# Row order in DRAM of the staged weight halves, and a three-dimensional source for their loads

## The reference

```python
for l in range(DEPTH):                       # DEPTH = 2
    mix = mixer_sublayer(h, ..., w_in[l], ..., w_out[l])
    h = layer_norm(DEEPNORM_ALPHA * h + mix, ln1_g[l], ln1_b[l])
    ffn = grouped_moe(h, router_w, router_bias, exp_w_gate[l], exp_w_up[l], exp_w_down[l])
    h = layer_norm(DEEPNORM_ALPHA * h + ffn, ln2_g[l], ln2_b[l])
...
for e in range(N_EXPERTS):                   # grouped_moe, 16 experts
    a = jax.nn.silu(h @ w_gate[e]) * (h @ w_up[e])
    y = y + dense_gates[:, e:e + 1] * (a @ w_down[e])
...
def swiglu(h, wi, wo):                       # four times in the second stack, D_FF = 2816
    gate, up = jnp.split(h @ wi, 2, axis=-1)
    return (jax.nn.silu(gate) * up) @ wo
```

## Time and profile before

| | |
|---|---|
| median of three runs | 2252.26 us |
| profiled execution, first to last instruction (span) | 2251.1 us |
| TensorE busy | 2131.1 us (95%) |
| VectorE busy | 1547.9 us (69%) |
| ScalarE busy | 1237.7 us (55%) |
| DMA traffic | 446.81 MB, 198 GB/s on average |
| the two expert stages, roughly | 225 to 496 us and 742 to 990 us of the span |

### The profile page before, as it was taken

One profiled execution on the slowest core, in us unless ns is written; L12 is line 12 of the kernel. 1 busy time (PEld: TensorE's weight loads), 2 busy tenths in 40 slices (PEclk: granted clock), 3 DMA queues, 4 the chain that ended last, 5 costly groups with the idle time before them and its releaser, 6 DMA issues.

```text
span 2251.1 us, 32506 instructions
## 1 busy us (share of the span) xinstructions
PE 2131.1 (95%) x12234; PEld 1855.9 (82%) x12234; DVE 1547.9 (69%) x2172; ACT 1237.7 (55%) x1985; POOL 50.0 (2%) x64
## 2 busy tenths in 40 slices
PE   7988999998988999989999998999999999889999
PEld 5777888876777788868999887789999997779998
DVE  7457999996557999985654757456666666655665
ACT  4454777764544777764444565544445444554443
POOL 0000000000000000010000000000000001000000
PEclk9999999998998999999999999999999999999999
DMA  6122999992224999975555452445565555133553
GB/s 240 64 76 96 354 360 361 364 355 98 86 78 143 366 360 358 361 292 169 168 187 188 157 182 95 149 131 176 184 194 177 180 187 197 66 121 131 187 186 114
DMA packets 124215, 446.81 MB, mean 198 GB/s; under 512 B 14320, under 2 KB 15472, under 8 KB 123120
## 3 DMA queue, kind: packets, MB, share of 16 engines
q1 hardware_dynamic: 124048, 444.61, 56.6%
HBM read 443.51 MB, written 1.05 MB: 197 GB/s over the span
## 4 chain that ended last, share of the span: by engine, by line
PE 49%; DVE 2%; ACT 2%; issue 1%; DMA 0%; POOL 0%; SPq 0%; DVEq 0%; ACTq 0%
PE bank L677 8%; PE bank L679 8%; PE bank L678 8%; PE bank L635 4%; PE bank L1074 4%; PE bank L1075 4%; PE bank L1076 4%; PE bank L636 4%; PE bank L637 4%; PE bank L2604 1%; PE bank L2586 1%; PE bank L947 1%; DMA scr<-in_alibi 0%; DVE lo L598 0%; ACT scr L3247 0%
## 5 line engine op out<-in xcount | busy, mean ns | idle before, releaser
L598 DVE TENSOR_TENSOR lo<-stage,hi 128x1024 fp32r<-128x1024 f32 (+1 forms) x834 | 969.6, 1205 | 252.4 <-ACT hi L586 225.3
L586 ACT ACTIVATE hi<-stage 128x1024 fp32r<-128x1024 f32 (+1 forms) x834 | 830.5, 1040 | 223.1 <-PE bank L637 88.5
L677 PE MATMUL bank<-thi,hi 128*128 128x256 f32 x1504 | 427.6, 284 | 5.1 <-DVE tlo L753 3.1
L679 PE MATMUL bank<-thi,lo 128*128 128x256 f32 x1504 | 426.2, 283 | 0.0
L678 PE MATMUL bank<-tlo,hi 128*128 128x256 f32 x1504 | 426.2, 283 | 0.0
L677 PEld LDWEIGHTS bank<-thi,hi 128*128 128x128 f32 x1504 | 289.1, 192 | 8.0 <-issue 6.5
L678 PEld LDWEIGHTS bank<-tlo,hi 128*128 128x128 f32 x1504 | 289.2, 192 | 1.4
L679 PEld LDWEIGHTS bank<-thi,lo 128*128 128x128 f32 x1504 | 289.1, 192 | 0.0
L635 PE MATMUL bank<-hi,thi 128*128 128x512 f32 (+3 forms) x656 | 261.2, 398 | 20.5 <-DVE tlo L753 7.5
L637 PE MATMUL bank<-hi,tlo 128*128 128x512 f32 (+3 forms) x656 | 254.4, 388 | 0.0
L636 PE MATMUL bank<-lo,thi 128*128 128x512 f32 (+3 forms) x656 | 254.3, 388 | 0.0
(11 more groups left out here) (369 smaller groups left out, 2748.2 us busy)
## 6 DMA issues: line engine op xcount, KB each, us to landing
stage<-in_exp SPq DMA_DIRECT2D x384, 512.0 KB, 5.3
stage<-in_ffn SPq DMA_DIRECT2D x264, 512.0 KB, 4.3
stage<-in_wi_a SPq DMA_DIRECT2D x16, 512.0 KB, 6.4
stage<-in_wi_b SPq DMA_DIRECT2D x16, 512.0 KB, 4.3
stage<-in_mem_wkv SPq DMA_DIRECT2D x16, 512.0 KB, 4.9
stage<-in_xwq SPq DMA_DIRECT2D x16, 512.0 KB, 4.0
stage<-in_xwo SPq DMA_DIRECT2D x16, 512.0 KB, 4.4
stage<-in_ssd_xbc SPq DMA_DIRECT2D x12, 512.0 KB, 4.1
```

The lines of the kernel that those rows point to most:

```text
L586: a.activation(self.hi[i % NR][:, x:y], self.stage[(2 * i + p) % (2 * NS)][:, :y - x], ACT.Copy).then_inc(*c.tick(("hi", i, p), sem="hi"))
L598: v.tensor_tensor(self.lo[i % NR][:, x:y], self.stage[(2 * i + p) % (2 * NS)][:, :y - x], self.hi[i % NR][:, x:y].bitcast(F32), ALU.subtra ...
L677: t.matmul(out, hi[:, ws], self.thi[:, xs], start=(k == 0), stop=False)
L679: m = t.matmul(out, lo[:, ws], self.thi[:, xs], start=False, stop=(k == 7))
```

## The change

It changes the order of the 128 rows of a half in DRAM to that of partitions 0, 8, 16, ..., 120, then 1, 9, 17, ..., 121, and so on to 7, 15, ..., 127. The load names the same 512 KB as a source of three dimensions, e (16, one row apart), j (8, 16 rows apart) and c (the row), so that partition 8e + j gets row 16j + e, which is its own row. The destination in SBUF, its contents, the number and size of the transfers, their order and their waits stay as they are.

```diff
 def halves(chunk):
 
-    x = chunk.reshape(128, -1)
-    n = x.shape[1] // 2
-    return x[:, :n].reshape(-1), x[:, n:].reshape(-1)
+    x = chunk.reshape(16, 8, -1).transpose(1, 0, 2)
+    n = x.shape[2] // 2
+    return x[:, :, :n].reshape(-1), x[:, :, n:].reshape(-1)
...
     def load(self, s, c, i):
         name, at, n = self.chunks[i]
         for p, (x, y) in enumerate(((0, n // 2), (n // 2, n))):
-            src = self.d[name][at + 128 * x:at + 128 * y].rearrange("(p c) -> p c", p=128)
+            src = self.d[name][at + 128 * x:at + 128 * y].rearrange("(j e c) -> e j c", j=8, e=16)
```

## The result

The changed kernel takes 2475.8 us (median of four runs, 2462.89 to 2486.13) beside 2254.41 us of the kernel before on the same chip, now in four runs: 1.098 times as long, with a 95% interval of 1.0933 to 1.1028. 2490 was predicted.

A forecast was written before the change was run, and what follows sets the result against it. The prediction took TensorE to bound the expert stages, with 3% of DMA room. It added 237 us for shared write destinations to the 2251.1 us span, all else nothing, for about 2490 us, range 2246 to 2620.

The forecast's parts named there:

- (a): SP's issue of a three-dimensional load: put at 0, range 0 to + 0.4 us per half, covered by the ring's slack.
- (b): Order in which DRAM is read for the stage loads: put at 0, a gain of at most 1.9 us.
- (c): Expert stages: DMA engines writing into one shared place at once, half the time, give 248 GB/s, + 237 us; chance 0.54.
- The sum: Whole kernel: span of 2251.1 us plus 237 us from the expert stages makes 2488, about 2490 us.
- The lower end: Expert stages if all engine pairs share all the time: 186 GB/s, 1009 us in place of 519, + 490 us.
- Feed-forward stages hide it: Feed-forward halves need 188 GB/s and get 248; their 4.3 us landing may grow by 1 us, hidden.
- Stage heads at nothing: Starts of stages, where TensorE waits for its operands anyway: no added time.
- The signs: Expert stages: slices below 300 GB/s, landings of 7 us and more, TensorE waiting for lo or hi every chunk, ScalarE for DMA.
- The hint of the 16-row table: A 128 KB load to 16 partitions took 97 GB/s, hinting that neighbouring partitions share a place with its own rate.
- no change: Rival for the whole kernel: engines keep writing as freely as today, 2252 us; chance 0.36.
- The costlier head: Rival at SP's issue and engine start: three dimensions delay each landing; + 1.3 us gives + 30 us, 2282; chance 0.06.
- faster reading: Rival at stage heads: adjacent rows read at one time land earlier, TensorE waits less, 2227 us; chance 0.04.

The follow-up runs named there:

- f1_group: Changed kernel with the 8 rows of each partition group adjacent in DRAM again, a gap keeping three dimensions: 2486.1 us (1.101).
- f2_pieces: Kernel before with stage loads in three dimensions on both sides, 128 partitions outermost, rows in two 2 KB pieces: 2254.7 us (1.0004).
- m2_stagger: Changed kernel's load form in streams without computation, small loads of n packets per part sent ahead of 40 loads: 235 to 389 GB/s.
- low2: Stream of loads without computation, form before (plain source) but 64 partitions of 8 KB, to partitions 0 to 63: 206 GB/s.
- low3: Stream of loads without computation, changed form (interleaved three-dimensional source) but 64 partitions of 8 KB, to partitions 0 to 63: 208 GB/s.
- mid3: Stream of loads without computation, changed form (interleaved three-dimensional source) but 64 partitions of 8 KB, to partitions 32 to 95: 415 GB/s.

## Why the prediction was right

The expert stages lost rate, as forecast, and that is nearly all of the time lost. That the total came within 15 us (2490 and 2475.8) is partly luck, since two errors of size in one product met.

- Work on the compute engines unchanged, no wait moved: right. The counts are the same, and the mean of a split too. TensorE's busy time grew from 2131.1 to 2181.4 us, VectorE's and ScalarE's by 1%, which the forecast put at nothing.
- (a), the issue hides: right in the outcome. It takes 0.54 us, 0.21 more than before, the middle of the 0 to 0.4 that it was given.
- (b), the read order gives and costs nothing: right, `f1_group`.
- (c), the engines' writes: right in kind, 263 GB/s in the expert stages for the 248 forecast. Of its sizes, the ceiling of today's form was put at 361 / 0.97 = 372 GB/s; the stream shows 410. A busy share of 0.97 did not mean that 3% of the ceiling was left but 12% (1 - 361 / 410): the engines read 1.02 at 410 GB/s, and 1.00 in `f2_pieces` went without any loss. The trace of the kernel before shows it as well, in slices of 5.75 us from 250 to 480 us, some of them over 400:

```profile
GB/s 383 380 336 382 393 341 377 395 368 325 353 360 320 328 415 398 368 353 375 385 354 358 337 336 363 316 405 331 411 348 400 408 376 312 338 344 383 318 397 380
```

- The sum takes 1.5 times the time per byte, from pairs of engines that share half of the time because they are out of step by half of a four-row run. No run shows the pairs or the run of four rows as such; the runs show, for loads all alike, 235 to 389 GB/s by the small loads ahead of them, with the peak at four packets of eight, and 263 GB/s in the stages. The share of one half was a choice for which no row spoke. By the forecast's own formula, from 413 alone to the 263 measured it is 413 / 263 - 1, 57%. With 372 and half the forecast had 248 GB/s, with 413 and 57% the runs have 263. Its reason, that nothing sets the engines in step, does not hold in the streams: with no distance added they run at 235 to 238, at the bottom of the curve of `m2_stagger`. The price of the two stages came to 213 us for 237.
- The lower end, 372 / 2 = 186 GB/s: partitions 0 to 63 gave 206 and 208 (low2, low3), half of 413 and 415, the forecast's end being low for the same reason. By this estimate the feed-forward stages would stay above their 188 even then.
- Feed-forward stages hide it: right, their landings grew from 4.3 to 5.6 us, where 1 us was allowed. By the prediction's own test, landings that had stayed at 4.3 would have spoken against the engines' rate as the cause; they did not stay.
- Stage heads at nothing: wrong by 8.3 us at the start of the program, right at the second mixer (0.0).
- The clock: 0.99 in both expert stages beside 1.00 before, though TensorE is idle for 78 of the 355 us of the first window, so it takes almost nothing.
- The signs: slices under 300 GB/s, landings over 7 us (9.3) and ScalarE waiting for DMA, as named. TensorE was to wait for lo or hi in every chunk; in 260 to 490 us, some 57 chunks, it waited 30 times for lo, twice for hi at the gate and up products and once at the down product, and 18 times for alo.
- The hint of the 16-row table came true: 97 GB/s were read from it, with two completions in the time, and the stream of 16 partitions gives 108. That the two are so near is luck in part.
- The rivals: no change (0.36) falls with the result, and with the 238 GB/s of the stream where the stages take 361. The 3% of room named against it was too small, but the fall in rate was larger than the true room. The costlier head falls with mid3, faster reading with `f1_group`.

## What to carry to other kernels

The form in which a source is named can set a load's rate: naming a source in three dimensions with 16 outermost cost 42% of the rate of a full stream to partitions 0 to 127 (410 to 238 GB/s), though bytes, length of the rows and destination were the same. Keep 128 outermost on both sides of a load to 128 partitions: that gave 410 GB/s in two dimensions, and in three, with pieces of 2 KB, 374 GB/s and no loss in the kernel. Whether such a thing matters is decided by the rate a stage takes: 188 GB/s hid it, 361 did not.

## What was not expected

- Small loads ahead of a stream moved its rate between 235 and 389 GB/s, and what they set lasted: 391 GB/s with 65 loads of 512 KB behind them, six in flight. The spread of the changed kernels' runs (about 1%) would fit a start that comes out differently each time; no run shows it.
- Single packets of the instruction queues may shift it: 391 became 378 GB/s, and 306 became 292, at one packet of 8 KB, while three other such packets changed nothing.
- 64 partitions can run as fast as 128 (413 GB/s at 32 to 95) or at half of that (206 at 0 to 63).
- The busy share of the DMA engines is a poor measure of room: 0.97 and 1.00 went with no loss at all, and 1.03 with 263 GB/s where the stages could take 361.
